# Embedding stage of a two-layer encoder: high weight parts on another engine, and the last layer finished token tile by token tile

## The reference

```
ple = sigmoid(h @ ple_gate[i]) * (p[i] @ ple_proj[i])      # (512x1024)(1024x1024), (512x256)(256x1024)
h = layer_norm(ALPHA * h + ple, ln_g[i, 3], ln_b[i, 3])    # (z - mean) * rsqrt(var + 1e-5) * g + b over 1024
```

## Time and profile before

| | us |
|---|---|
| median of 3 runs | 3105.27 (3102.4 to 3106.46) |
| profiled execution | 3102.91 |
| its span | 3101.1 |
| PE busy | 2999.5 (97%) |
| POOL busy | 2344.7 (76%) |
| DVE busy | 1362.0 (44%) |
| ACT busy | 635.1 (20%) |

### The profile page before, as it was taken

One profiled execution on the slowest core, in us unless ns is written; L12 is line 12 of the kernel. 1 busy time (PEld: TensorE's weight loads), 2 busy tenths in 40 slices (PEclk: granted clock), 3 DMA queues, 4 the chain that ended last, 5 costly groups with the idle time before them and its releaser, 6 DMA issues.

```text
span 3101.1 us, 47691 instructions
## 1 busy us (share of the span) xinstructions
PE 2999.5 (97%) x20178; PEld 2449.0 (79%) x20178; DVE 1362.0 (44%) x1765; ACT 635.1 (20%) x1031; POOL 2344.7 (76%) x1877
## 2 busy tenths in 40 slices
PE   8999999989999999999899999999999999999996
PEld 7888877777778888888788888777777788888884
DVE  4221233765637462211762213238565555622127
ACT  1000124643310020000310002354432100200021
POOL 8988796742259989988899987867331799898875
PEclk9999999999999999999999999999999999999998
DMA  4332242111113333333233323422110233333322
GB/s 135 101 102 96 89 129 69 51 50 34 30 55 95 122 102 102 96 101 95 89 96 103 100 96 95 121 61 58 37 36 23 69 101 124 100 104 95 96 88 88
DMA packets 201488, 266.60 MB, mean 86 GB/s; under 512 B 12305, under 2 KB 130429, under 8 KB 201277
## 3 DMA queue, kind: packets, MB, share of 16 engines
q1 hardware_dynamic: 194624, 243.51, 25.8%
q10 hardware_dynamic: 6652, 20.05, 1.7%
HBM read 257.22 MB, written 6.29 MB: 85 GB/s over the span
## 4 chain that ended last, share of the span: by engine, by line
PE 83%; POOL 8%; DVE 5%; issue 2%; ACT 1%; DMA 0%; POOLq 0%; SPq 0%; DVEq 0%; ACTq 0%
PE ps L852 70%; POOL w_lo L1178 4%; POOL w_hi L1175 4%; PE ps L404 1%; PE ps L422 1%; PE ps L416 1%; PE ps L1051 1%; PE ps L1029 1%; PE ps L1045 1%; PE ps L1058 1%; PE ps L899 1%; PE ps L1098 1%; PE ps L486 0%; DVE hT_lo L1674 0%; PE ps L381 0%
## 5 line engine op out<-in xcount | busy, mean ns | idle before, releaser
L1175 POOL TENSOR_TENSOR w_hi<-w_raw,zero 128x512 fp32r<-128x512 f32 (+2 forms) x936 | 1085.3, 1159 | 649.9 <-PE ps L852 607.9
L1178 POOL TENSOR_TENSOR w_lo<-w_raw,w_hi 128x512 fp32r<-128x512 f32 (+2 forms) x936 | 1286.6, 1375 | 73.2
L852 PE MATMUL ps<-hT_hi,w_hi 128*128 128x512 f32 (+1 forms) x2368 | 927.7, 392 | 14.1 <-POOL w_lo L1178 11.4
L852 PE MATMUL ps<-hT_hi,w_lo 128*128 128x512 f32 (+1 forms) x2368 | 905.7, 382 | 0.0
L852 PE MATMUL ps<-hT_lo,w_hi 128*128 128x512 f32 (+1 forms) x2368 | 905.5, 382 | 0.0
L852 PEld LDWEIGHTS ps<-hT_hi,w_hi 128*128 128x128 f32 x2368 | 443.9, 187 | 123.8 <-POOL w_lo L1178 21.8
L852 PEld LDWEIGHTS ps<-hT_hi,w_lo 128*128 128x128 f32 x2368 | 443.7, 187 | 89.2
L852 PEld LDWEIGHTS ps<-hT_lo,w_hi 128*128 128x128 f32 x2368 | 444.2, 188 | 84.4 <-issue 2.9
L1746 DVE TENSOR_TENSOR act_raw<-silu,ps 128x512 f32<-128x512 f32 x88 | 59.9, 681 | 616.9 <-PE ps L852 616.9
L852 PE MATMUL ps<-w_hi,aT_hi 128*128 128x512 f32 x704 | 274.6, 390 | 0.0
L852 PE MATMUL ps<-w_lo,aT_hi 128*128 128x512 f32 x704 | 273.9, 389 | 0.0
(11 more groups left out here) (305 smaller groups left out, 3530.5 us busy)
## 6 DMA issues: line engine op xcount, KB each, us to landing
w_raw<-in_w_in SPq DMA_DIRECT2D x104, 512.0 KB, 3.6
w_raw<-in_ffn_wg SPq DMA_DIRECT2D x176, 256.0 KB, 2.8
w_raw<-in_ffn_wu SPq DMA_DIRECT2D x176, 256.0 KB, 3.1
w_raw<-in_ffn_wd SPq DMA_DIRECT2D x88, 512.0 KB, 3.6
w_raw<-in_w_in SPq DMA_DIRECT2D x96, 128.0 KB, 2.3
w_raw<-in_w_out SPq DMA_DIRECT2D x16, 512.0 KB, 3.7
w_raw<-in_ple_gate SPq DMA_DIRECT2D x16, 512.0 KB, 3.7
ln_rows<-in_ln_g ACTq DMA_DIRECT2D x8, 512.0 KB, 3.9
```

The lines of the kernel that those rows point to most:

```text
L852: ins = nc.tensor.matmul(o, l_, r_, start=first, stop=last, skip_group_check=into is not None)
L1175: nc.gpsimd.tensor_tensor(w_split[0][:, q, kk, 0:w], w_raw[:, r, kk, 0:w], zero[:, 0:1].to_broadcast([P, w]), ALU.add).then_inc(*step("w_h ...
L1178: nc.gpsimd.tensor_tensor(w_split[1][:, q, kk, 0:w], w_raw[:, r, kk, 0:w], w_split[0][:, q, kk, 0:w].bitcast(F32), ALU.subtract).then_inc( ...
```

## The change

Six slots of each layer's embedding stage (`pproj` of both halves and the four of `pgate` half 1) get their high parts from ScalarE, by a copy to fp32r, at places written out in ScalarE's order; GpSimd waits for each and makes the low part. In the last layer TensorE takes `pgate` half 1 and `pproj` half 1 together (`tiles_in_turn`): slots 0 and 1 of the gate for all tiles, then gate and projection tile by tile. The last norm has no separate scaling on ScalarE: VectorE makes (z - mean) * gain in one pass of 128x1024 in place, and times 1/deviation plus bias in two passes of 128x512 in place, each half stored by itself (256 KB, eight stores). The two rows are loaded ahead of the last sigmoids. In the layer norms of other stages `first_norms` and `rows_of` are only pieces of the former `norm`, called in the same order.

```diff
+        act_slots = {(g[0], i): n for n, (_, g, i) in enumerate(slot_list)
+                     if g[0][0] == "pproj" or (g[0][0] == "pgate" and g[0][2] == 1)}
...
+            def tiles_in_turn(L):
+
+                gate, g0, _, n_tiles = open_group(("pgate", L, 1), hT, False, lambda m: ("ple_sig", L, 1, m), every)
+                proj, p0, _, _ = open_group(("pproj", L, 1), pT, False, lambda m: ("ple_mul", L, 1, m), every)
+                for i in range(2):
+                    for kk in range(2):
+                        pe.wait_ge(*after("w_rest_ready", g0 + i, kk))
+                        for m in range(n_tiles):
+                            gate(i, kk, m)
+                for group, m in (("g", 0), ("g", 1), ("p", 0), ("p", 1), ("g", 2), ("p", 2), ("g", 3), ("p", 3)):
+                    for i in (2, 3) if group == "g" else (0,):
+                        for kk in range(2):
+                            if m == 0:
+                                pe.wait_ge(*after("w_rest_ready", (g0 if group == "g" else p0) + i, kk))
+                            (gate if group == "g" else proj)(i, kk, m)
...
+                    elif L < DEPTH - 1:
+                        run(dense(("pgate", L, half), hT, False, lambda m: ("ple_sig", L, half, m)))
                     else:
-                        run(dense(("pgate", L, half), hT, False, lambda m: ("ple_sig", L, half, m)))
+                        tiles_in_turn(L)
+                        continue
                     run(dense(("pproj", L, half), pT, False, lambda m: ("ple_mul", L, half, m), tail=1))
...
-                    nc.gpsimd.tensor_tensor(w_split[0][:, q, kk, 0:w], w_raw[:, r, kk, 0:w], zero[:, 0:1].to_broadcast([P, w]),
-                                            ALU.add).then_inc(*step("w_high", n, kk))
-                    pool.wait_ge(*after("w_high", n, kk))
+                    if (g[0], i) in act_slots:
+                        pool.wait_ge(*after("w_high_act", n, kk))
+                    else:
+                        nc.gpsimd.tensor_tensor(w_split[0][:, q, kk, 0:w], w_raw[:, r, kk, 0:w], zero[:, 0:1].to_broadcast([P, w]),
+                                                ALU.add).then_inc(*step("w_high", n, kk))
+                        pool.wait_ge(*after("w_high", n, kk))
...
+            def rows_of(L, q):
 
                 now(*{0: ("dense_done", "down", L, 0, 1, 3), 1: ("dense_done", "out", L, 1, 3),
                       2: ("dense_done", "down", L, 1, 1, 3), 3: ("h_scaled", L, 2, NT - 1)}[q])
                 act.dma_start(ln_rows[:, 0, :], a["ln_g"][L, q:q + 1, :].partition_broadcast(P)).then_inc(*step("rows_in", L, q, by=16))
                 act.dma_start(ln_rows[:, 1, :], a["ln_b"][L, q:q + 1, :].partition_broadcast(P)).then_inc(*step("rows_in", L, q, by=16))
...
+            def high_parts(name, i):
+
+                n = act_slots[(name, i)]
+                now(f"w_in{n % RAW_RING}", n)
+                now(*slot_free[n - SPLIT_RING])
+                for kk in range(2):
+                    nc.scalar.activation(w_split[0][:, n % SPLIT_RING, kk, :], w_raw[:, n % RAW_RING, kk, :], ACT.Copy).then_inc(
+                        *step("w_high_act", n, kk))
+
+            def embedding_gate(L, half, m):
+                now("dense_done", "pgate", L, half, m)
+                if half:
+                    now("ple_mul", L, 0, m)
+                nc.scalar.activation(ple_sig[:, m, :], ps[banks_of.get(("pgate", L, half, m), 0)][:, :], ACT.Sigmoid).then_inc(
+                    *step("ple_sig", L, half, m))
...
                 norm(L, 2)
+                high_parts(("pproj", L, 0), 0)
+                high_parts(("pgate", L, 1), 0)
+                for m in range(4):
+                    embedding_gate(L, 0, m)
+                for i in range(1, 4):
+                    high_parts(("pgate", L, 1), i)
+                high_parts(("pproj", L, 1), 0)
+                if L == DEPTH - 1:
+                    rows_of(L, 3)
+                    for first in (0, 2):
+                        for m in (first, first + 1):
+                            embedding_gate(L, 1, m)
+                        for m in (first, first + 1):
+                            deviation_of(L, 3, m)
+                else:
+                    for m in range(4):
+                        embedding_gate(L, 1, m)
+                    first_norms(L, 3)
+                    norm(L, 3)
+            for t in range(NT):
                 for half in range(2):
-                    for m in range(4):
-                        now("dense_done", "pgate", L, half, m)
-                        if half:
-                            now("ple_mul", L, 0, m)
-                        nc.scalar.activation(ple_sig[:, m, :], ps[banks_of.get(("pgate", L, half, m), 0)][:, :], ACT.Sigmoid).then_inc(
-                            *step("ple_sig", L, half, m))
-                norm(L, 3, last=L == DEPTH - 1)
-
-            for t in range(NT):
-                now("h_final", t)
-                act.dma_start(out[0, t * P:(t + 1) * P, :], h_new[:, t % 2, :]).then_inc(*step(f"stored{t % 2}", t, by=16))
-            now("stored0", NT - 2)
-            now("stored1", NT - 1)
+                    now("h_final", t, half)
+                    cols = slice(512 * half, 512 * half + 512)
+                    act.dma_start(out[0, t * P:(t + 1) * P, cols], h_tok[:, t, cols]).then_inc(*step("stored", t, half, by=16))
+            now("stored", NT - 1, 1)
...
+            def last_norm(L, q, t):
+
+                stats(L, q, t, 1)
+                now("bn_done", L, q, t, 1)
+                v.bn_aggr(ln_mv[:, t, :], ln_small[:, t, 0:12]).then_inc(*step("ln_var", L, q, t))
+                now("ln_var", L, q, t)
+                now("rows_in", L, q)
+                v.scalar_tensor_tensor(h_tok[:, t, :], h_tok[:, t, :], ln_mv[:, t, 0:1], ln_rows[:, 0, :], ALU.subtract, ALU.mult)
+                now("ln_sqrt", L, q, t)
+                chain(v.reciprocal(ln_rstd[:, t, :], ln_rstd[:, t, :]))
+                for half in range(2):
+                    cols = slice(512 * half, 512 * half + 512)
+                    v.scalar_tensor_tensor(h_tok[:, t, cols], h_tok[:, t, cols], ln_rstd[:, t, :], ln_rows[:, 1, cols], ALU.mult,
+                                           ALU.add).then_inc(*step("h_final", t, half))
...
-                        if half:
+                        if half == 0:
+                            stats(L, 3, m, 0)
+                        elif L == DEPTH - 1:
+                            last_norm(L, 3, m)
+                        else:
                             normalise(L, 3, m)
-                        else:
-                            stats(L, 3, m, 0)
-                norm(L, 3, last=L == DEPTH - 1)
+                if L < DEPTH - 1:
+                    norm(L, 3)
```

More of the change, by code:

```diff
@@ L197, in build @@
                 h_raw = sb(o2, "h_raw", [P, KD, SEQ])
-                h_new = sb(o2, "h_new", [P, 2, D])
                 ple_sig = sb(o2, "ple_sig", [P, 4, 512])
@@ L1307, in norm, with first_norms @@
                 act.dma_start(ln_rows[:, 1, :], a["ln_b"][L, q:q + 1, :].partition_broadcast(P)).then_inc(*step("rows_in", L, q, by=16))
+            def first_norms(L, q):
+                for t in range(2):
+                    deviation_of(L, q, t)
+                    normalised(L, q, t)
+            def norm(L, q):
+                deviation_of(L, q, 2)
+                features(L, q, 0, 0)
+                features(L, q, 0, 1)
+                normalised(L, q, 2)
+                features(L, q, 0, 2)
+                features(L, q, 0, 3)
+                deviation_of(L, q, 3)
+                normalised(L, q, 3)
+                for k in range(4):
+                    features(L, q, 1, k)
+                for k in range(4, KD):
+                    now("hT_x", L, q, 1, k)
+                    nc.scalar.activation(hT[0][:, k, :], h_raw[:, k, :], ACT.Copy).then_inc(*step("hT_raw", L, q, 1, k))
+                rows_of(L, q)
                 if q == 1:
                     act.dma_start(p_tok[:, :, :], a["p"][L, 0].rearrange("(t p) d -> p t d", p=P)).then_inc(*step("p_in", L, by=16))
+            def high_parts(name, i):
[11 more added lines that the diff above has]
+                    *step("ple_sig", L, half, m))
             def ffn(L, f):
@@ L1474, in _ @@
                 ffn(L, 0)
+                first_norms(L, 0)
                 norm(L, 0)
@@ L1631, in _ @@
                     act.dma_start(h_tok[:, t, :], h_dram[t, :, :]).then_inc(*step("h_back", L, by=16))
+                first_norms(L, 1)
                 norm(L, 1)
                 ffn(L, 1)
+                first_norms(L, 2)
                 norm(L, 2)
-                for half in range(2):
-                    for m in range(4):
-                        now("dense_done", "pgate", L, half, m)
-                        if half:
-                            now("ple_mul", L, 0, m)
```

(23 more changed lines are left out.)

## The result

| | before | changed |
|---|---|---|
| median, us | 3105.2 (3102.4 to 3106.46, 4 runs) | 3081.81 (3081.35 to 3082.27, 4 runs) |
| ratio | | 0.9926, 95% interval 0.9909 to 0.9943 |
| span of the profiled execution | 3101.1 | 3080.2 |

The account below looks back on a forecast made before the run. TensorE waiting for GpSimd's splitting, then a VectorE tail, was taken as the bound. Last stage -13.7 and layer 0 -5.0 make -18.7 us: 3084.2 profiled, 3086.6 median, range 3080.5 to 3093.5.

Parts of the forecast that it names:

- TensorE unstalled: Last stage: TensorE never waits after the first `pproj` slot starts and reaches the last slot for tile 0 96 products later.
- The hand-over at nothing: ScalarE's high parts handed to GpSimd cost nothing: last slot ready at 3057.1 to 3058.8, wanted by TensorE at 3059.2.
- VectorE's tile: Last stage: a tile with the fused norm takes VectorE 5.25 us (5.0 to 5.8), four take 21.0.
- Root and sigmoid in turn: Last stage: ScalarE's table switches between square root and sigmoid stay hidden, by 0.6 us at tile 2.
- Stores: End of last stage: 2.1 MB queue at 360 GB/s takes 5.8 us after a fixed 1.3, last landing 3086.6.
- Layer 0: Embedding stage of layer 0: VectorE starts 3.8 us earlier and tile 1 runs clean, 1.2 more; 5.0 us in all.
- Rival C: High parts do not set when the last `pproj` slot starts; gain only 4.4 us, 3100.9; chance 0.05.
- 3084.2 lies 2.4 under the median: Final step from profiled execution to median of runs: the 2.4 us distance of the kernel before added to 3084.2, giving 3086.6.

Follow-up runs that it names:

- high_only: Kernel before, with only the high parts of the six slots of each layer moved to ScalarE, order and last norm as before: 3093.64 us, ratio 0.9969.
- no_turns: Changed kernel with the last stage's gate and projection groups one after the other, as before: 3089.01 us, ratio 0.9954.
- no_high: Changed kernel with all high parts back on GpSimd, tile by tile order and fused norm kept: 3099.82 us, ratio 0.9986.
- old_norm: Changed kernel with the last norm in its old form (scaling on ScalarE, two passes after all four tiles, whole-tile stores), rows still loaded early: 3087.0 us, ratio 0.9944.
- proj_sooner: Changed kernel with TensorE's order gate 0, projection 0, gate 1, projection 1 and so on: 3081.64 us, ratio 0.9924.

## Why the prediction was right

**TensorE unstalled: right.** P1 for tile 0 was put 96 products after P0 and stood there. `high_only` and `no_turns` split it: the copies bring VectorE's start 4.0 us forward (30.7 us after the first sigmoid, for 34.7), the order by tiles 5.45 more, and `no_high` shows that the second needs the first.

**The hand-over at nothing: right.** P1's low parts were ready 1.5 us ahead, within the forecast 0.4 to 2.1.

**VectorE's tile: right, 0.11 too long.** 5.14 for 5.25: the first pass is the 1.28 taken, but the next operation starts 1.21 after it, and the half passes take 1.33 for 1.37. The four tiles took 20.65 for 21.0.

**Root and sigmoid in turn: right here, by a margin that `old_norm` shows to be thin.** 0.5 us of cover for 0.6 forecast.

**Stores: the term mis-sized in the last stage.** Predicted last stage 3087.4 - 3035.5 = 51.9, measured 50.37. Of the 1.5 about 0.6 are there before the first store: VectorE's start, 0.3 earlier from the first sigmoid, and three tiles. The other 0.9 lie between tile 3's root and the end, 7.0 us for 7.9. Of these, 0.4 is the rate: 2.1 MB at 385 GB/s, where I took 360, between one window of larger rows and the weight queue's mean. Another 0.3 is that ScalarE issues the first store as the root starts (3072.91), not when it is done, and 0.2 is left in the fixed parts.

**Layer 0: 5.5 for 5.0.** VectorE's start came 4.1 forward against 3.8. Tile 1 ran clean as forecast, 3.0 for 4.1 before, and tile 0, which I had left at the earlier trace rows's 4.2, took 3.85: 1.5 where I had 1.2.

**Rival C's number was right, as `no_high`.** It had the last stage 4.4 shorter with P1 late, and it is 4.46: the tail's form alone. That the two agree so closely is partly luck: the tail was 5.2 shorter, and VectorE started 0.7 later.

**Of the 4.8 us beyond the forecast, 2.0 are of the change.** They are the 0.5 and 1.5 above; 0.2 is from stages outside. The remaining 2.6 is the step "3084.2 lies 2.4 under the median": I carried the distance of one profiled execution over to the other kernel. There it was 3082.0 against 3081.81, none. With mixers that wander by 5 us such a distance is chance, so 2.6 of the 23.4 us were neither foreseen nor are they shown to come from the change.

The sum of the last stage closes: -4.0 (copies) - 5.45 (order) - 5.7 (tail, from tile 0's start to the end: 30.9 to 25.1) = -15.2. The copies alone gave 4.15 (`high_only`), order and tail without them 4.46 (`no_high`).

**Open.** The lengths of the mixers and the two lengths of the seam go with the time that the granted clock stood at 0.50; why it falls or comes back at a given place in one execution and not in another is not shown. In mixer 0 the first difference seen lies at TensorE's wait for four small loads, which landed 2.6 to 3.2 us (median) after issue in the four traces compared; no run tests whether the one leads to the other. Nor does the clock account for all: mixers with the same time at 0.50 still differ by up to 2.3 us.

## What to carry to other kernels

Where a helper engine holds up TensorE, first free the helper, then reorder: the order by tiles was worth 5.4 us behind the copies and nothing without them. Compare traces stage by stage between marks that no edit touches; a 3 us effect disappears in the span and stands out to a tenth in its stage. Where a stage without an edit differs, read its granted clock first: here it tells most of the difference. When two engines alternate inside a loop, price the order of the second one too: both of my larger misses (`old_norm`, `proj_sooner`) were a place in ScalarE's queue.

## What the runs showed of the hardware

TensorE's granted clock went from 1.00 to 0.50 in `no_high` after a stretch in which it was busy 0.97 of 2 us with three matmuls, and matmuls went from 0.227 to 0.43 us apart until about 3070; in the kernel before, with single waits of 1.2 to 1.3 us between whole slots, it stayed at 1.00. Small pieces with a wait at each were dearer here than the waits, by up to 1.6 us at P1. In mixer 0, TensorE waited 2.45 us in the kernel before and 2.33 in the changed one, and the clock fell only in the second: the same wait need not have the same price in every execution. And stores of 2 KB rows ran at 385 GB/s at full share, near the 390 taken from the earlier trace rows with 4 KB rows.
